# FFN down product of a two-block transformer kernel: seven of eight block products in two column halves, and modulation chunks spread over other stages

## The reference

```python
def conv_ffn(x, norm_g, w_up, conv_w, conv_b, w_down):        # D_FF = 2816, CONV_W = 3
    u = rmsnorm(x, norm_g) @ w_up                            # 1024 -> 2 * 2816
    c = conv_b + sum over j of up[:, j:j + s_] * conv_w[j]   # along the tokens, causal
    val, gate = jnp.split(c, 2, axis=-1)
    return (jax.nn.silu(gate) * val) @ w_down                # 2816 -> 1024

    mod = silu(c) @ w_ada[l] + b_ada[l]                      # 1024 -> 3 * 1024: shift, scale, gate
    h = rmsnorm_2(x, g_pre[l]) * (1.0 + scale) + shift
    ...
    x = x + gate * rmsnorm_2(y, g_post[l])
```

## Time and profile before

| | |
|---|---|
| median of 3 runs | 962.8 us (962.21 to 964.73) |
| the profiled execution, its own time | 964.29 us |
| its span, first to last instruction | 962.5 us |
| PE busy | 952.1 us, 99% of the span |
| DVE busy | 710.4 us, 74% |
| ACT busy | 273.9 us, 28% |
| 16 DMA engines | 171.98 MB moved, mean 179 GB/s |

### The profile page before, as it was taken

One profiled execution on the slowest core, in us unless ns is written; L12 is line 12 of the kernel. 1 busy time (PEld: TensorE's weight loads), 2 busy tenths in 40 slices (PEclk: granted clock), 3 DMA queues, 4 the chain that ended last, 5 costly groups with the idle time before them and its releaser, 6 DMA issues. The chain is left out here.

```text
span 962.5 us, 15687 instructions
## 1 busy us (share of the span) xinstructions
PE 952.1 (99%) x5928; PEld 863.8 (90%) x5928; DVE 710.4 (74%) x1614; ACT 273.9 (28%) x597; POOL 0.7 (0%) x7
## 2 busy tenths in 40 slices
PE   9999999999999999999999999999999999999997
PEld 8888999999999988888999999999888878888876
DVE  4768877776887478757677778875699971899963
ACT  1032112112111222264121121112534453624561
POOL 0000000000000000000000000000000000000000
PEclk9999999999999999999999999999999999999999
DMA  8940565756675230664267566752643413433101
GB/s 321 406 174 8 220 194 220 267 216 243 246 271 221 77 142 1 240 252 171 116 229 271 201 255 244 270 212 88 251 154 131 164 45 113 183 133 101 55 1 44
DMA packets 33811, 171.98 MB, mean 179 GB/s; under 512 B 4696, under 2 KB 8544, under 8 KB 17504
## 3 DMA queue, kind: packets, MB, share of 16 engines
q1 hardware_dynamic: 32096, 168.25, 46.8%
q10 hardware_dynamic: 1664, 3.04, 0.9%
HBM read 170.21 MB, written 2.64 MB: 180 GB/s over the span
## 5 line engine op out<-in xcount | busy, mean ns | idle before, releaser
L1304 PE MATMUL bank<-work,fring 128*128 128x256 f32 x704 | 155.7, 380 | 1.2 <-DVE work L2183 1.2
L1304 PEld LDWEIGHTS bank<-work,fring 128*128 128x128 f32 x704 | 132.2, 190 | 18.8 <-issue 2.0
L2157 DVE SCALAR_TENSOR_TENSOR work<-work,cols 128x256 f32<-128x256 f32 x176 | 71.6, 479 | 53.3 <-ACT work L658 53.3
L2383 DVE SCALAR_TENSOR_TENSOR work<-work,cols 128x256 f32<-128x256 f32 x240 | 98.8, 479 | 1.0 <-ACT work L832 0.5
L1291 PE MATMUL bank<-sq,fring 128*128 128x128 f32 x640 | 84.6, 275 | 0.0
L1291 PE MATMUL bank<-sq,ring 128*128 128x128 f32 x640 | 78.0, 275 | 0.0
L1291 PE MATMUL bank<-ring,fring 128*128 128x128 f32 x640 | 78.0, 275 | 0.0
L1291 PEld LDWEIGHTS bank<-sq,fring 128*128 128x128 f32 x640 | 77.9, 192 | 0.0
L658 ACT ACTIVATE work<-work,cols 128x256 f32<-128x256 f32 x88 | 45.6, 589 | 113.0 <-DVE work L2136 97.4
L1291 PEld LDWEIGHTS bank<-ring,fring 128*128 128x128 f32 x640 | 76.2, 192 | 1.0
L1291 PEld LDWEIGHTS bank<-sq,ring 128*128 128x128 f32 x640 | 74.7, 192 | 0.0
(11 more groups left out here) (395 smaller groups left out, 1577.4 us busy)
## 6 DMA issues: line engine op xcount, KB each, us to landing
ring<-in_ring SPq DMA_DIRECT2D x60, 1024.0 KB, 6.4
fring<-in_up SPq DMA_DIRECT2D x44, 1024.0 KB, 6.7
work<-in_ada SPq DMA_DIRECT2D x48, 512.0 KB, 5.7
fring<-in_down SPq DMA_DIRECT2D x22, 1024.0 KB, 4.9
ring<-in_ring SPq DMA_DIRECT2D x2, 800.0 KB, 5.2
bias_skewed<-bias_rows SPq DMA_DIRECT2D x1, 1536.0 KB, 13.6
consts<-in_consts ACTq DMA_DIRECT2D x1, 1128.0 KB, 15.2
ring<-in_ring SPq DMA_DIRECT2D x2, 512.0 KB, 4.7
```

Of the source, the lines that this page charges most:

```text
L1304: last = mm(pb[m // 2][:, T * (m % 2):T * (m % 2 + 1)], w[:, k, P * m:P * (m + 1)], f_act[:, par, T * k:T * (k + 1)], start=(first and k = ...
L2157: ins = v.scalar_tensor_tensor(f_t[q][:, c, :], f_u[:, q, c, tap:tap + T], col(f"f_conv_w{f}", 44 * tap + n), f_t[q][:, c, :], ALU.mult, A ...
L2383: marks[c] = link(v.scalar_tensor_tensor(b_y[:, c, :], b_a[:, c, tap:tap + T], col("conv_w_2", 124 * l + 4 * tap + c), b_y[:, c, :], ALU.m ...
```

## The change

**Down product.** The 1024 output columns are done in two halves ("groups") of 512. For each group and step the product of the 256 hidden features and 512 outputs is taken as seven products of half-size blocks: 7 x 2 matmuls of 128 columns. Group 0 is done in the loop, in banks 0 to 3; group 1 after it, in banks 4 to 7, with its own pass over all 11 steps, for which the activations of all steps are kept (`f_x`). DVE makes the sums of the weights (`down_sums`, per group and step, three instructions of 256, 512 and 256 columns) and the differences of the activations (`gated`, three further instructions of 256, 128 and 128 columns); `down_out` puts a group's products together. `products_out` is now called per column half, with `s_forms` between the two.

**Modulation.** The 48 chunks are no longer computed 24 in each FFN. One is done in every FFN step (11), one after each of four `down_sums` of the second pass (4), one in each of the heads 1 to 6 of the first block's attention (6), and twelve at the end of layer 0 of the second block: 2 + 4 before the first `y2_conv`, 2 before the second, 4 behind it. They are numbered 0 to 47: 15 to 20 are in the attention and 36 to 47 at the end of layer 0. Their pieces (`ada`) go through three buffers of their own; the load of chunk n waits until chunk n - 3 has been computed, and the loads stand in SP's program where the diff shows.

Smaller edits: the silu of c is done once; the transfer of the position bias is issued later; two of four `spread` matmuls of the mLSTM stage come after two score products.

```diff
+        ada_w = sb("ada_w", [P, 3, D])
...
+            def load_down(f, group, i, first=False):
+
+                if group == 0 and not first:
+                    sp.wait_ge(S("down_done"), down_no(f, 0, i - 2))
+                if group == 1:
+                    if i < 4:
+                        sp.wait_ge(S("up_done"), FF_STEPS * f + 10 + i // 2)
+                    else:
+                        sp.wait_ge(S("down_done"), down_no(f, 1, i - 4))
+                at = 1024 * (FF_STEPS * group + i)
+                sp.dma_start(down_place(f, group, i)[:, 256:1280], I["down"][f][:, at:at + 1024])\
+                    .then_inc(S(down_landed(f, group, i)[0]), 16)
+
+            def load_ada(first, last):
+
+                for n in range(first, last):
+                    if n >= 3:
+                        sp.wait_ge(S("ada_free"), n - 2)
+                    at = D * (n % 24)
+                    sp.dma_start(ada_w[:, n % 3, :], I["ada"][n // 24][:, at:at + D]).then_inc(S(f"ada{n % 3}"), 16)
...
+                for i in range(3, FF_STEPS):
+                    load_up(f, i, (FF_STEPS * f + i) % 2)
+                    load_down(f, 0, i - 1)
+                    load_ada(a + i, a + i + 1)
+                load_down(f, 1, 0)
+                load_down(f, 1, 1)
+                load_down(f, 0, FF_STEPS - 1)
+                for i in range(2, FF_STEPS):
+                    load_down(f, 1, i)
+                    if 3 <= i < 7:
+                        load_ada(a + 8 + i, a + 9 + i)
+                load_ada(a + 15, a + 18)
...
+            sp.dma_start(c_row[:, :], I["c_2"][0].partition_broadcast(P)).then_inc(S("c_in"), 16)
+            load_ada(0, 3)
...
             sp.wait_ge(S("tok_out"), 20)
             for i in (0, 1):
                 load_up(1, i, 1 - i)
-                load_down(1, i, 1 - i)
+                load_down(1, 0, i, True)
+            load_ada(18, 24)
             for n in range(32, 36):
...
+                    for n in range(48, 52):
+                        load(n)
+                    load_ada(39, 48)
+                    for n in range(52, 64):
...
+                def down(group, i):
+
+                    pe.wait_ge(S("down_sums"), down_no(f, group, i))
+                    if group == 0:
+                        pe.wait_ge(S("act_ready"), g0 + i + 1)
+                    elif i == 0:
+                        pe.wait_ge(S("u_ready"), 2 * (g0 + FF_STEPS))
+                    s1, vlo, glo, ghi, vhi, s2, s3, s4 = down_parts(f, group, i)
+                    x11, t3, x21, x22, t0, t2, t1 = [f_x[i][:, P * j:P * j + P] for j in range(7)]
+                    one, two, three_, four = [pb[b] for b in DOWN_BANK[group]]
+                    for n, (bank, at, w, x) in enumerate(((one, 0, vlo, x11), (four, 0, s2, t1), (four, T, vhi, x21),
+                                                          (two, 0, s1, t0), (two, T, s3, t2), (three_, 0, s4, x22),
+                                                          (three_, T, ghi, t3))):
+                        for c in range(2):
+                            last = mm(bank[:, at + P * c:at + P * (c + 1)], w[:, P * c:P * (c + 1)], x,
+                                      start=(i == 0 and at == 0 and c == 0), stop=(i == FF_STEPS - 1),
                                       skip_group_check=True)
+                        if i == FF_STEPS - 1 and n < 6:
+                            last.then_inc(S("down_part"), 1)
                     last.then_inc(S("down_done"), 1)
 
+                up_plain(g0, g0 % 2, g0 // 2 + 1, xg_ready(8 + 16 * f), lambda: ss(nth + 1, pb[0][:, 0:T]))
+                for i in range(1, FF_STEPS):
+                    up(g0 + i, (g0 + i) % 2, first=(i == 1))
+                    down(0, i - 1)
+                down(1, 0)
+                down(1, 1)
+                down(0, FF_STEPS - 1)
+                for i in range(2, FF_STEPS):
+                    down(1, i)
...
+            def ada(count):
+
+                for n in range(ada_at[0], ada_at[0] + count):
+                    dve.wait_ge(S(f"ada{n % 3}"), 16 * (n // 3 + 1))
+                    x, l, j = ada_w[:, n % 3, :], n // 24, n % 24
+                    v.scalar_tensor_tensor(x, x, 1.0, c_row[:, :], ALU.mult, ALU.mult, accum_out=mod[:, l, j:j + 1])\
+                        .then_inc(S("ada_free"), 1)
+                ada_at[0] += count
...
+                def down_sums(group, i):
+
+                    dve.wait_ge(S(down_landed(f, group, i)[0]), down_landed(f, group, i)[1])
+                    w = down_place(f, group, i)
+                    s1, vlo, glo, ghi, vhi, s2, s3, s4 = down_parts(f, group, i)
+                    then(v.tensor_tensor(s1, glo, ghi, ALU.add))
+                    then(v.tensor_tensor(w[:, 1280:1792], w[:, 0:512], w[:, 256:768], ALU.subtract))
+                    v.tensor_tensor(s4, vhi, s2, ALU.subtract).then_inc(S("down_sums"), 1)
...
+                def gated(i, conv):
+
+                    x = f_x[i]
+                    dve.wait_ge(S("silu_done"), 2 * (g0 + i) + 2)
+                    after(conv)
+                    then(v.tensor_tensor(x[:, 0:512], f_sg, f_t[0].rearrange("p a b -> p (a b)"), ALU.mult))
+                    then(v.tensor_tensor(three(x[:, 512:768], 2), three(x[:, P:P + 512], 2)[:, :, 0:P],
+                                         three(x[:, 0:2 * P], 2), ALU.subtract))
+                    then(v.tensor_tensor(x[:, 768:896], x[:, 384:512], x[:, 512:640], ALU.subtract))
+                    v.tensor_tensor(x[:, P:2 * P], x[:, 256:384], x[:, 768:896], ALU.subtract)\
                         .then_inc(S("act_ready"), 1)
...
+                def down_out(group):
+
+                    part, c = 12 * f + 6 * group, 4 * group
+                    one, two, three_, four = [pb[b] for b in DOWN_BANK[group]]
...
+                    dve.wait_ge(S("down_p1"), 2 * f + group + 1)
+                    n_low = link(v.tensor_tensor(low, low, three(d_p1, 2), ALU.add))
+                    dve.wait_ge(S("down_part"), part + 3)
+                    then(v.tensor_tensor(d_u2, d_p1, four[:, 0:T], ALU.add))
+                    after(n_low)
+                    v.tensor_tensor(low, low, three(four[:, T:2 * T], 2), ALU.add)
+                    dve.wait_ge(S("down_part"), part + 5)
+                    then(v.tensor_tensor(d_u43, d_u2.unsqueeze(1).broadcast_to([P, 2, T]), three(two[:, :], 2), ALU.add))
+                    n_mid = link(v.tensor_tensor(middle, middle, d_u43.rearrange("p a (b t) -> p a b t", b=2), ALU.add))
+                    then(v.tensor_tensor(high, high, three(d_u43[:, 1, :], 2), ALU.add))
+                    v.tensor_tensor(high, high, three(two[:, 0:T], 2), ALU.add)
+                    dve.wait_ge(S("down_done"), down_no(f, group, FF_STEPS - 1))
+                    after(n_mid)
+                    v.tensor_tensor(middle, middle, three_[:, :].rearrange("p (a b t) -> p a b t", a=2, b=2), ALU.add)\
+                        .then_inc(S("h_ready"), 2)
...
+                for i in range(FF_STEPS):
+                    g = g0 + i
+                    if i == 0:
+                        plain_out(g)
+                    else:
+                        products_out(g, 0)
+                        if i + 1 < FF_STEPS:
+                            s_forms((g + 1) % 2, (g + 1) // 2 + 1)
+                        else:
+                            down_sums(1, 0)
+                            down_sums(1, 1)
+                        products_out(g, 1)
+                    down_sums(0, i)
+                    taps(i, 0)
+                    conv = taps(i, 1)
+                    ada(1)
+                    gated(i, conv)
+                if f == 1:
+                    modulation(0)
+                    layer_gains(0)
+                    v.memset(rstd[:, T:T + 1], 1.0)
+                    v.tensor_copy(xr[:, :, T:T + 1], mod[:, 0, 0:DC].unsqueeze(2))
+                down_sums(1, 2)
+                down_sums(1, 3)
+                down_out(0)
+                for m in range(2):
+                    down_sums(1, 4 + m)
+                    onward(m)
+                for i in range(6, FF_STEPS):
+                    down_sums(1, i)
+                    if i < 10:
+                        ada(1)
+                down_out(1)
+                for m in range(2, 4):
+                    onward(m)
...
-            attention(0, A_DH ** -0.5, lambda n: pc("mask_ts", DIAG))
-            layer_gains(0)
+            attention(0, A_DH ** -0.5, lambda n: pc("mask_ts", DIAG), lambda n: ada(1) if 1 <= n < 7 else None)
...
+                if l == 0:
+                    ada(2)
...
+                if l == 0:
+                    ada(4)
                 dve.wait_ge(S("conv_gate"), l + 1)
                 for m in range(2):
                     if m == 0:
                         dve.wait_ge(S("pw2_first"), l + 1)
                     else:
+                        if l == 0:
+                            ada(2)
```

(71 more changed lines are left out.)

229 lines of the change are left out of this document (93 added, 136 removed).

## The result

The changed kernel took 983.1 us (979.5 to 985.1, 4 runs) where the kernel before, on the same chip, took 963.3: ratio 1.0195, 95% interval 1.0169 to 1.0222. It is slower, by 1.7 to 2.2%. Forecast were 975 and a range of 964 to 983, so the sign and the two large stalls were right, and the size was 8 us short: the time lies at the upper edge of the range, 0.1 us over it.

A forecast was written before the change was run, and what follows sets the result against it. PE, busy 99% of the span, was taken as the bound. From the profiled 964.3 us: - 15.6 + 2.6 + 1.7 + 9.4 + 12.0 + 2.5 = 976.9, median 975.4, stated as 975; range 964 to 983 (8 in 10).

The forecast's parts named there:

- Down product: Both FFNs: calls of 28 narrow instructions take 3.13 us each; with an idle wait removed, 15.6 us gained.
- the two large stalls: PE waits on late modulation chunks: 9.4 us in head 4 of the attention, 12.0 us at the end of layer 0.
- Second pass: Group 1 of the FFNs: piece 7, queued behind chunk a + 14, comes late; 1.0 and 1.6 us, together 2.6.
- Transition: From group 1 to the next stage: DVE's last sums in `down_out(1)` hold PE 0.85 us per FFN, together 1.7.
- Attention: Head 4: chunk 18 lands behind FFN 1's six pieces, so PE waits 9.4 us, plus 1.8 at half pace.
- End of layer 0: Chunks from 39 on wait behind `load(51)`, delaying both `y2_conv`: 12.0 us, plus 0.7 at half pace.
- Half pace after idling: PE runs slowly behind both stalls: 1.8 us in the attention, 0.7 at the end of layer 0, together 2.5.
- The prediction's own sentence on the bias: The moved position bias lands tens of us before its use, so it was priced at nothing.
- transfers are served side by side: Rival: chunk 18 lands about when DVE asks, the end of layer 0 saves 1 us; median 964, chance 0.08.
- DVE is the bound: Rival: DVE limits the FFN loops, beside the two waits; 975 us plus up to 18, chance 0.07.
- its threshold of 16.0 us a step: FFN loops: DVE's step, estimated at 15.1 us, must exceed 16.0 before DVE rather than PE limits them.
- neither wait comes: Rival: chunks 18 and 39 have landed when DVE asks, so both waits and half pace vanish; median 951.5, chance 0.09.

The follow-up runs named there:

- fix_all: Changed kernel with four re-orderings of SP's issues together (attention, end of layer 0, second pass, start of FFN 0): 952.4 us, ratio to before 0.9895.
- fix_tail: Changed kernel with modulation chunk a + 14 issued behind the eighth piece of the second pass instead of ahead of it: 979.9 us, ratio to before 1.0175.
- attn_half: Changed kernel with chunks 18 to 20 issued between FFN 1's first pair of pieces and its second: 972.5 us, ratio to before 1.0109.
- experiment 10: Also written `warm_end`: changed kernel with 44 unused identity products on PE before its wait for layer 0's first `y2_conv`: 985.1 us, ratio to before 1.0228.
- fix_start: Changed kernel with only chunk 0 issued before FFN 0, chunks 1 and 2 behind its third up pair: 978.5 us, ratio to before 1.0159.
- the repeat: The changed kernel run once more with nothing altered, on the chip of the runs beside it: 982.6 us, ratio to before 1.0200.

## Why the prediction was right, and where it fell short

- **Down product: right.** A call takes 3.13 us as computed, 22 of them per FFN. Where nothing else is in the way (`fix_all`) the two FFNs are 8.0 and 7.9 us shorter, 15.9 for the 15.6 forecast. The ratio of the Trainium skill ("TensorE: Matmul & The Clock Gate", section "Back-to-back issue gap") that the prediction weighed against narrow products, 81 ns instead of 56, does not show in these float32 instructions: 28 in 3.13 us are 0.112 us each, as in the earlier trace rows.
- **Second pass: right in place, 0.6 us too large.** 0.87 and 1.09 us were lost to a + 14's place (`fix_tail` removes both); 1.0 and 1.6 were forecast.
- **Transition: right.** 0.9 us after each FFN, forecast 0.85 each. It stays in every version.
- **Attention: right.** DVE went on with chunk 18 at 442.08, forecast 440.8 with a start 1.3 us earlier; PE idled 9.19, forecast 9.4; with the slow products behind it 11.3 us, forecast 11.2. `attn_half` shows that the landing follows the bytes ahead.
- **End of layer 0: right in cause, 1.0 us too small.** 13.7 us, 12.7 forecast with the clock's part. Counted from the product of piece 43, the second `y2_conv` came 13.6 us later than in before, where 12.0 was forecast: `load(51)` landed after 4.7 us instead of 4.1, and chunk 43, issued when chunk 40 was done, after 4.8 where a lone piece's 3.8 was taken. With five chunks ahead of `load(51)` 2.2 us stay (`fix_all`).
- **Half pace after idling: right in kind, wrong in place.** It came behind both stalls. In the attention it cost 1.9 us, 1.8 forecast; at the end of layer 0, where 0.7 was forecast, it cost 0.1, since all of the slow stretch lay in the wait for the second `y2_conv` (experiment 10). The two together are 2.0 for the 2.5 forecast.
- **The step that failed: what is moved ahead of FFN 0.** The prediction has no term for c_row and `load_ada(0, 3)`; it followed the chunks' issues at the two places where they stood behind something, and not what stands behind them: the bias, and the third up pair. It cost 1.93 us of idle time and 1.7 of slow products in the profiled execution (`fix_start`: 4.6 us by the medians, 3.9 in FFN 0's stage); in the repeat and the five other kernels that keep this order it was 1.1 to 2.3 us of idle time and no slow products. The prediction's own sentence on the bias is of another transfer, the load of the prepared bias, which the change moved and for which nothing waited; the one in the way is the copy before it, which stands where it stood, but now behind 2 MB more.
- **Start-up: not forecast, in part not explained.** 4.7 us in the profiled execution up to the first L1109 product, 0.2 to 1.9 in the other eleven, and the changed kernel's times spread over 5.5 us where the four of before beside them spread over 2.5; two larger sets of before spread over 6, so the spread alone shows nothing. The move of `spread` gave back 1.2, which I had at nothing.

Together, on the profiled executions: 976.9 forecast + 3.7 (start of FFN 0) + 3.5 (start-up less `spread`) + 1.0 (end of layer 0) + 0.2 (attention, transitions) - 0.3 (down) - 0.6 (second pass) = 984.4, measured 985.05.

The rivals: that transfers are served side by side fell with `attn_half`. The prediction's own ground against it was none, since the last transfer issued lands last, when all the bytes are through, either way. The landings of the four up pieces that before issues from 423.43 to 425.5 (L373) would have been one: issued within 2.1 us of each other, they landed 5.0 to 14.1 us later, the last some 11 us behind the first.

```profile
DMA to landing us min/median/max: 5.0/9.7/14.1
```

That DVE is the bound fell, with 0.40 us to spare, though its threshold of 16.0 us a step was too high: at 15.96 the kernel already lost 10 us. The threshold rested on DVE being done with `s_forms` 3.4 us before PE asks; in `fix_all` it is done at 205.85 and PE's next `up` starts at 207.4. That neither wait comes is what `fix_all` is: forecast 951.5 for it, measured 952.4, in part because two terms cancel: the forecast holds 2.6 us for the second pass, which this version doesn't lose, and nothing for the 2.2 that stay at the end of layer 0.

## What to carry to other kernels

When work moves to where an engine has idle time, follow its transfers through the issuing queue, both ways: what does each stand behind (an event, or bytes), and what now stands behind it. Here 30 us were lost to an order of issues whose repair is a few lines, in a change whose arithmetic gained what was computed. And price a stall from the timeline, as the gap plus the slow products behind it, but leave out slow products that end in another wait: at the end of layer 0 they cost nothing. The distances between the same products before and after give the price without this question. Differences of medians, each with its own start-up, added up to 35.6 us where 30.2 were gained.

## What was not expected of the hardware

- Half pace came after idle times as short as 1.93 us (167 us: 16 products in 2.35 and 16 in 2.96 instead of 1.79; the granted clock 0.76 in 167 to 170 and 0.75 in 170 to 174) and 2.41 us (28.87, 16 products in 3.54), and did not come after 1.75 at the same place in the repeat, 2.30 there in `warm_end`, 2.47 in `attn_half`, or 2.13 at the start (8.72, 24 products of 256 columns in 5.42, the full pace). The length of the gap alone doesn't tell.
- While the copy of the position bias (1.5 MB) is on its way the rate is low, in the changed kernel as in before (244 GB/s at a DMA share of 0.86 in 137 to 146 us there), although the DMA engines are busy, so what is behind it pays for more than its bytes. That the copy itself is what slows them was not tested apart. The windows of the changed kernel, ahead of it and in it (last two columns: DMA share, GB/s):

```profile
142.00:149.00 7.00, 7.00 (x34) 6.16 (x33) 6.79 (x15) 2.29 (x2) 0.00 (x0) 1.00 0.97 356
149.00:156.00 7.00, 7.00 (x62) 6.94 (x61) 6.54 (x16) 3.08 (x7) 0.00 (x0) 1.00 1.09 215
```
